# A hybrid decoder step on one core: tile 1's output matmuls spread over the query jobs, and the last tile's sums finished by halves of the columns

## The chip, the cores and the metric

The kernel runs on one core of a Trainium2 chip. The time is that of one execution on the device, in microseconds (us), median of three. A core has TensorE (PE, matmuls; PEld is its weight loads), VectorE (DVE), ScalarE (ACT), GpSimd (POOL), SyncE (SP, which here only issues DMAs), and sixteen DMA engines that all queues share. Engines run their own instruction lists in order and meet at semaphores.

## What is computed

A hybrid decoder layer (attention and a state-space branch) for 512 prompt tokens and 8 sample tokens, followed by a product-key expert layer. Only its second half is touched by the change:

```python
yp = yp + mp                      # mp, ms: output projection m @ w_out of the mixer
ys = ys + ms
yp = yp + _peer(_rmsnorm(yp, norm_ffn[l]), peer_w_q[l], peer_keys1[l], peer_keys2[l], peer_u[l], peer_v[l])
ys = ys + _peer(_rmsnorm(ys, norm_ffn[l]), ...)
y_prompt = _rmsnorm(yp, norm_final)
y_sample = _rmsnorm(ys, norm_final)

# _peer, for a token: 8 heads, 2 x 128 keys
q = (hc @ w_q).reshape(PEER_CHUNK, PEER_HEADS, PEER_QDIM)
s1, s2 = scores of the two halves of q with the two key tables
v1, i1 = lax.top_k(s1, 16);  v2, i2 = lax.top_k(s2, 16)
sc, ci = lax.top_k(all 256 sums v1 + v2, 16)
e = i1[ci // 16] * 128 + i2[ci % 16]          # 128 expert rows a token
g = softmax(sc)
out = sum over e of g * gelu(u_tab[e] . hc) * v_tab[e]
```

## The kernel before

Tokens lie in five tiles of 128: tiles 0 to 3 are the prompt, tile 4 the eight samples. Two stages matter, each a block with its own semaphores and closed by a barrier of all engines (`open_block`, L95). The order inside a block is written out by hand: each engine runs a Python function that emits its instructions, and where a piece goes is set by small constants such as `OUT_AT`.

**stage_route** (L1667) works on tiles 0 and 1. `out(n)` on TensorE is one half of columns of the output projection of one tile: n = 0, 1 are tile 0, n = 2, 3 tile 1, eight matmuls each (two instructions a matmul in the trace, L1788). VectorE's `add(n)` (L1919) puts it onto the residual y1. ScalarE squares a tile (`square`, L1849) and takes the root (`root`), VectorE's `variance` and `scale` (L1929) give the normed h. `turn(t)` transposes it (L1800), ScalarE's `keep_turned` (L1858) copies it to hT. Then come 28 jobs, `JOBS`, each a query matmul group (`queries`, L1812) and scores against the keys (L1831), with copies by ScalarE (L1845). There are 16 half heads (hh). Jobs 0 to 11 are half heads of tile 0 alone, jobs 12 to 15 are of both tiles together (256 wide), jobs 16 to 27 of tile 1 alone. VectorE takes the best 16 of each half head of tile 0 (`best16`, L1587 to L1594) in the loop `for hh in range(HH)`, and after each of the `PORTIONS` the best 16 sums (`choose_best`, L1604). The indices of all but the last portion are worked out on POOL (L1724 to L1737), the last by VectorE (`choose_index`, L1619 to L1629). When all are there, ScalarE takes exponents (job `EXP_AT`), VectorE normalises (L1637 to L1639), TensorE turns indices and gates (`turn_choice`, behind job `CHOICE_AT`), ScalarE stores them in idxT and gateT (L1652, L1653), and POOL issues the first four gathers of expert rows (L1744). ScalarE, POOL and VectorE also split h into three bf16 parts (`split_high`, `split_middle`, L1712, L1714, L1970, L1972), which SP stores to h_split (`store_rows`, L1759) for the next stage. SP loads the weights of the queries (L1501), and at the end two pieces of late weights (L1773) and the gain of the norm (L1775).

**stage_experts** takes 130 batches. A batch is four gathers by POOL (L2097), each of 128 rows of 8 KB (u and v of an expert), the broadcast of h (L2203), four dot products on VectorE (L2462), a gelu on ScalarE, weights (`weights`, L2356), and sixteen matmul instructions that sum the v rows into acc (`combine`, L2309): the first eight fill columns 0 to 511, the others 512 to 1023. The routing of tiles 2 to 4 is done between the batches in the first half of this stage. When a tile is through, `finish` (L2366 add, L2369 variance, L2375 scaling) and ScalarE's `square` and `root` (L2503, L2507) give its output, and SP stores it (L2110; L2114 for the samples, batches 128 and 129).

Of the kernel before, what the change touches and what calls it, by code (L numbers as in the profile page):

```python
# [21 lines left out]
ALU = mybir.AluOpType  # L22
ACT = mybir.ActivationFunctionType
# [7 lines left out]
P = 128  # L31
D = 1024
KT = D // P
# [6 lines left out]
TILES = 5  # L40
# [9 lines left out]
EPS = 1e-6  # L50
# [14 lines left out]
TOPK = 16  # L65
# [1599 lines left out]
def stage_route(nc, io, S):  # L1665
# [3 lines left out]
    PORTIONS = ((0, 2), (2, 2), (4, 2), (6, 1), (7, 1))  # L1669
# [3 lines left out]
    OUT_AT, SQUARE_AT, ROOT_AT = 3, 5, 6  # L1673
    TURN_AT = 7
    EXP_AT, CHOICE_AT = 21, 26
    with ExitStack() as ctx:
# [27 lines left out]
        def _(pool):  # L1704
# [12 lines left out]
            for i, (first, count) in enumerate(PORTIONS[:-1]):  # L1717
                pool.wait_ge(E["halved"], i + 1)
                n = count * TOPK
                f = R.fi[:, 2:2 + 2 * count].rearrange("p (h w) a -> p h w a", w=2)  # L1720
                hit = R.hit[:, 0:count]
                terms = hit.rearrange("p h k a -> p (h k) a")
                hl, hf, pick = (x[:, :, TOPK:TOPK + n] for x in (R.hl, R.hf, R.pick))
                link(pool.tensor_copy(R.fi[:, 2:2 + 2 * count], R.iu[:, 0, 2 * first:2 * (first + count), :]))  # L1724
# [23 lines left out]
        def _(sp):  # L1748
# [13 lines left out]
            for c in range(4, len(JOBS) // 2):  # L1762
                sp.wait_ge(E["q_done"], 2 * (c - 3))
                load_route(sp, io, S, c)
                if c == 6:
                    store_rows(0)
                if c == 8:
                    sp.wait_ge(E["stored"], 16)
                    sp.wait_ge(E["normed"], EARLY)
                    load_rows(sp, S, 0, S.first_rows)  # L1770
            sp.wait_ge(E["done"], 2 * EARLY)
# [4 lines left out]
            store_rows(1)  # L1776
# [3 lines left out]
        def _(pe):  # L1780
# [42 lines left out]
            out(2, 4, KT)  # L1823
            for j, (hh, t0, t1) in enumerate(JOBS):
# [9 lines left out]
                if j == OUT_AT:  # L1834
                    out(3)
# [8 lines left out]
        def _(act):  # L1844
# [37 lines left out]
            for j, (hh, t0, t1) in enumerate(JOBS):  # L1882
# [21 lines left out]
                if j == CHOICE_AT - 1:  # L1904
                    split_middle(1)
# [6 lines left out]
        def _(dve):  # L1912
# [29 lines left out]
            for hh in range(HH):  # L1942
                dve.wait_ge(E["s_kept"], kept_by[hh] + 1)
                best16(dve, link, [(R.v[:, 0, hh, :], R.iu[:, 0, hh, :], s[:, hh, :])])
                for i, (first, count) in enumerate(PORTIONS):
                    if hh == 2 * (first + count) - 1:
# [7 lines left out]
                        hl = R.hl[:, :, TOPK:TOPK + n]  # L1954
# [3 lines left out]
                if hh == 0:  # L1958
                    add(2)
                if hh == OUT_AT:  # L1960
                    add(3)
# [13 lines left out]
def stage_experts(nc, io, S):  # L1975
# [12 lines left out]
    with ExitStack() as ctx:  # L1988
# [13 lines left out]
        ss = sb("ss", [P, TILES + LATE])  # L2002
# [10 lines left out]
        ss2, rstd2 = ss[:, TILES:], rstd[:, TILES:]  # L2013
# [20 lines left out]
                 "h_stored", "room_free", "moved")  # L2034
# [153 lines left out]
        def _(pe):  # L2188
# [108 lines left out]
            def combine(B):  # L2297
# [7 lines left out]
                for h in range(2):  # L2305
                    for c in range(BATCH):
# [5 lines left out]
                                         start=(r == 0), stop=(r == (LANE if n < TILES - 1 else LAST_B) - 1))  # L2312
                last.then_inc(E["v_used"], 1)
# [31 lines left out]
        def _(dve):  # L2345
# [148 lines left out]
            weights(len(batches) - 1)  # L2494
            finish(TILES - 2, 2)
            for part in range(3):
                finish(TILES - 1, part)

        @block.scalar
        def _(act):  # L2500
# [103 lines left out]
            square(TILES - 1)  # L2604
# [202 lines left out]
```

## Time and profile before

| | us |
|---|---|
| median of 3 runs | 2030.96 (2028.79 to 2032.86) |
| the profiled execution's own time | 2034.55 |
| its span, first to last instruction | 2032.8 |
| stage_route, from its first matmul to the experts' first | 505.9 to 618.9 |
| stage_experts | 618.9 to 2032.8 |

Busy shares over the whole span are PE 76%, DVE 64%, POOL 33%, ACT 14%. They mix stages with different limits; the stage in question has to be read from its own stretch. In the rows below, a line of a timeline is: start, duration, engine, line of the kernel, operation, tensors, shapes, count, and in brackets how long the engine had been idle and what ended that. POOL's DMA_INDIRECT rows are the time to issue a gather, not to move it.

### The profile page before, as it was taken

The page shows a single profiled execution, that of the slowest core. Times are in us where ns is not written, and L with a number is a line of the kernel's source. Part 1 is how long each engine was busy: PE and PEld are TensorE (multiplying, and loading weights), DVE is VectorE, ACT ScalarE, POOL GpSimd, SP SyncE. Part 2 cuts the span into 40 slices and gives each one's busy share as a digit, 9 for nine tenths or more (in the row PEclk, how much of TensorE's full clock was granted, in tenths as well). Part 3 has the DMA queues.
Part 4 walks back from the last instruction along what each step waited for, and adds up shares of the span by engine and source line. Part 5 has one row for each costly group of instructions (what it writes and reads, how often), then busy time and mean ns, then how long its engine had stood idle before and what let it go on. Part 6 is the DMA issues. An engine that isn't in the chain of part 4 may idle for free.

```text
span 2032.8 us, 22490 instructions
## 1 busy us (share of the span) xinstructions
PE 1548.4 (76%) x7517; PEld 684.5 (34%) x7517; DVE 1295.6 (64%) x3113; ACT 294.3 (14%) x723; POOL 677.9 (33%) x832
## 2 busy tenths in 40 slices
PE   6999789999986888886787866665666666666665
PEld 5447575637683445441343411110001111111110
DVE  5999627532475787745577896458886445454545
ACT  3001135421222222201111101000000000000000
POOL 4930003400283333233332333333333333333332
PEclk9999787999997888996777866556666555666656
DMA  5322433364669999999999999999999999999997
GB/s 190 104 82 87 135 102 127 111 252 160 216 226 382 421 413 407 412 413 418 413 374 414 393 401 413 422 414 414 406 403 420 413 418 414 415 415 410 418 414 293
DMA packets 141591, 668.59 MB, mean 329 GB/s; under 512 B 17252, under 2 KB 50724, under 8 KB 71524
## 3 DMA queue, kind: packets, MB, share of 16 engines
q0 software_dynamic: 74880, 545.29, 65.5%
q1 hardware_dynamic: 66596, 121.85, 17.5%
q8 instruction: 61, 1.00, 0.2%
q14 instruction: 54, 0.44, 0.1%
HBM read 659.95 MB, written 19.65 MB: 334 GB/s over the span
## 4 chain that ended last, share of the span: by engine, by line
DMA 32%; PE 19%; DVE 8%; issue 7%; POOL 3%; ACT 0%; DVEq 0%; POOLq 0%; ACTq 0%
DMA ex_uv<-in_peer_uv,idxT 20%; DMA w_out<-in_peer_uv,idxT 12%; PE ex_acc L2309 10%; PE ex_hb L2203 4%; DVE ex_uv L2462 2%; POOL ex_uv L2097 2%; PE ex_late L2228 2%; POOL w_out L2097 1%; PE ex_late L2276 1%; DVE w_out L2462 1%; PE ex_pick L2228 1%; PE ex_late L2243 1%; DVE ch_iu L1590 1%; PE ex_late L2256 1%; DVE ch_ci L1590 1%
## 5 line engine op out<-in xcount | busy, mean ns | idle before, releaser
L2203 PE MATMUL ex_hb<-ffn_gain,spread 24*128 24x512 bf16 x1040 | 355.8, 505 | 404.5 <-DVE ex_uv L2462 260.9
L2462 DVE SCALAR_TENSOR_TENSOR ex_uv<-ex_uv,ex_hb 128x1024 f32<-128x1024 f32 x344 | 416.3, 1219 | 312.9 <-DMA ex_uv<-in_peer_uv,idxT 278.8
L2097 POOL DMA_INDIRECT ex_uv<-in_peer_uv,idxT x344 | 325.4, 946 | 612.7 <-PE ex_acc L2309 523.0
L2462 DVE SCALAR_TENSOR_TENSOR w_out<-w_out,ex_hb 128x1024 f32<-128x1024 f32 x176 | 213.1, 1219 | 164.7 <-DMA w_out<-in_peer_uv,idxT 123.6
L2203 PEld LDWEIGHTS ex_hb<-ffn_gain,spread 24*128 24x128 bf16 x1040 | 54.0, 99 | 740.1 <-DVE ex_uv L2462 398.5
L2309 PE MATMUL ex_acc<-ex_uv,wts 128*32 128x512 f32 x1376 | 276.3, 946 | 0.0
L2097 POOL DMA_INDIRECT w_out<-in_peer_uv,idxT x172 | 161.5, 939 | 297.5 <-PE ex_acc L2309 258.2
L2592 ACT ACTIVATE ex_gelu<-ex_dots 128x4 f32<-128x4 f32 x130 | 26.7, 205 | 1087.3 <-DVE ex_uv L2462 725.8
L2309 PE MATMUL ex_acc<-w_out,wts 128*32 128x512 f32 x704 | 139.9, 938 | 0.8 <-DVE wts L2356 0.8
L2309 PEld LDWEIGHTS ex_acc<-ex_uv,wts 128*32 128x32 f32 x1376 | 47.7, 147 | 160.3 <-issue 160.3
L756 POOL TENSOR_TENSOR at_prob<-at_prob,at_coef 128x256 f32<-128x256 f32 (+3 forms) x32 | 40.1, 1253 | 120.6 <-DVE at_coef L866 120.5
L2276 PE MATMUL ex_late<-hx,sgT 128*128 128x264 f32 x256 | 67.9, 423 | 0.0
L1812 PE MATMUL ro_pq<-hT,w_q 128*128 128x128 f32 (+1 forms) x448 | 61.3, 290 | 0.8 <-ACT hT L1858 0.8
L1812 PEld LDWEIGHTS ro_pq<-hT,w_q 128*128 128x128 f32 x448 | 56.8, 192 | 3.4 <-issue 2.0
L2276 PEld LDWEIGHTS ex_late<-hx,sgT 128*128 128x128 f32 x256 | 51.9, 208 | 16.8 <-issue 7.1
L2309 PEld LDWEIGHTS ex_acc<-w_out,wts 128*32 128x32 f32 x704 | 24.4, 147 | 85.2 <-issue 82.7
L2228 PE MATMUL ex_late<-hx,sgT 128*128 128x264 f32 x128 | 39.1, 471 | 9.1 <-DVE ex_small L2394 9.1
L297 DVE TENSOR_TENSOR vc<-pr_x,pr_tab 128x512 f32<-128x512 f32 x64 | 43.0, 731 | 0.6
L624 PE MATMUL pr_yp<-vc,pr_c_pad 128*32 128x256 f32 x256 | 35.4, 425 | 8.8 <-DVE vc L297 8.8
L297 DVE TENSOR_TENSOR pr_x<-pr_bu,pr_tab 128x512 f32<-128x512 f32 x64 | 39.6, 678 | 1.2 <-PE pr_bu L611 1.2
L1705 POOL MEMSET y<- 128x1024 f32 x1 | 1.0, 952 | 110.6 <-POOLq L99 110.6
L572 PE MATMUL pz<-gate_ring,vc 128*128 128x512 f32 (+1 forms) x96 | 36.6, 534 | 0.0
(500 smaller groups left out, 2177.7 us busy)
## 6 DMA issues: line engine op xcount, KB each, us to landing
sgT<-in_late_w SPq DMA_DIRECT2D x24, 1024.0 KB, 9.1
w_q<-in_peer_w_q SPq DMA_DIRECT2D x14, 1024.0 KB, 6.3
gate_ring<-in_w_in SPq DMA_DIRECT2D x6, 2048.0 KB, 9.5
ex_uv<-in_peer_uv,idxT POOLq DMA_INDIRECT x344, 13.6
ks_rows<-in_ks_pages SPq DMA_DIRECT2D x64, 64.0 KB, 2.2
vs_rows<-in_cache_v_sel SPq DMA_DIRECT2D x64, 64.0 KB, 2.1
vc<-in_vc_pages SPq DMA_DIRECT2D x64, 64.0 KB, 2.1
gate_ring<-in_kc_pages SPq DMA_DIRECT2D x64, 64.0 KB, 2.1
```

What stands on the lines that cost most here:

```text
L297: tt = lambda o_, x_, y_, op: dve.tensor_tensor(o_, x_, y_, op)
L572: last = pe.matmul(ps[j % 3][0:m_, 0:n], of, ring[:, c % 2, k, 0:n], start=(k == 0), stop=(k == KT - 1))
L624: last = pe.matmul(yp[strip(n), (p // 2) % 2, 0:SPAN], c_pad[:, part, n, :], zb[:, s % 2, j, e, :], start=(j == 0), stop=(j == 3))
L756: pool.tensor_tensor(prob[:, b, :, 0:n], prob[:, b, :, 0:n], coef[:, b, :].unsqueeze(2).broadcast_to([P, NKV, n]), ALU.mult).then_inc(E["s ...
L1590: ins = dve.max_index(idx[:, part], vals[:, part], x)
L1812: last = pe.matmul(pq[:, j % 2, P * t0:P * t1], w[:, c % 4, k, P * m:P * m + P], S.hT[:, k, P * t0:P * t1], start=(k == 0), stop=(k == KT ...
L2097: pool.indirect_dma_start(slot(s).rearrange("p j n -> p (j n)"), None, table, bass.IndirectOffsetOnAxis(ap=S.idxT[:, t:t + 1], axis=0))\
L2203: last = pe.matmul(hb[s % 2][:, CHUNK * h:CHUNK * h + CHUNK], spread[p, k % LOAD, :], h_rows[p, l % 2, CHUNK * h:CHUNK * h + CHUNK], start ...
L2228: last = pe.matmul(bank[i][:, 0:LATE_TOK], w[:, k, col], S.hx[:, k, :], start=(k == 0), stop=(k == KT - 1))
L2276: last = pe.matmul(late[:, 0:LATE_TOK], w[:, k, P * (j % 2):P * (j % 2) + P], S.hx[:, k, :], start=(k == 0), stop=(k == KT - 1))
L2309: last = pe.matmul(acc[LANE * g:LANE * g + LANE, CHUNK * h:CHUNK * h + CHUNK], wts[:, s % (2 * BATCH), LANE - 1 - r:2 * LANE - 1 - r], slo ...
L2462: dve.scalar_tensor_tensor(out=rows_, in0=rows_, scalar=1.0, in1=hb[s % 2][:], op0=ALU.mult, op1=ALU.mult, accum_out=dots[:, B % 2, c:c + ...
```

## The change

In stage_route:

- The last two portions, of one head each, become one of two heads: POOL works out three portions, VectorE the indices of the last two heads. The scratch buffers that POOL uses start two heads further on, since VectorE's own part needs two.
- out(2)'s second half goes behind job 3, out(3)'s halves behind jobs 5 and 7 (before: out(2)'s second half ahead of the second query, all of out(3) behind job 3). VectorE adds them behind half heads 4 and 7 (before 0 and 3).
- The square of tile 1 moves from job 5 to 9, the root from 6 to 10, the transposes (`TURN_AT`) from behind job 7 to behind job 10, next to the first job that needs them. The variance and scaling on VectorE follow.
- The exponents go from job 21 to 19, the turn of the choice from 26 to 22. The middle part of tile 1's split goes from job 25, one ahead of the choice, to job 23, one behind it.
- SP stores tile 1's split ahead of the two late weight pieces and the gain, not behind them.

In stage_experts, at the very end: the samples' last sum is added in two halves of 512 columns, the first as soon as the first eight matmul instructions are through (new semaphore `half_used`), both ahead of tile 3's scaling. ScalarE squares each half into its own column of ss, and VectorE puts the two sums together in two small steps.

```diff
-    PORTIONS = ((0, 2), (2, 2), (4, 2), (6, 1), (7, 1))
+    PORTIONS = ((0, 2), (2, 2), (4, 2), (6, 2))
...
-    OUT_AT, SQUARE_AT, ROOT_AT = 3, 5, 6
-    TURN_AT = 7
-    EXP_AT, CHOICE_AT = 21, 26
+    OUT_AT = {3: (2, 4, KT), 5: (3, 0, 4), 7: (3, 4, KT)}
+    SQUARE_AT, ROOT_AT, TURN_AT = 9, 10, 10
+    EXP_AT, CHOICE_AT = 19, 22
...
# SyncE, end of stage_route
                     load_rows(sp, S, 0, S.first_rows)
+            store_rows(1)
             sp.wait_ge(E["done"], 2 * EARLY)
             for p in range(2):
                 sp.dma_start(S.late_ring[:, p, :], io["late_w"][p]).then_inc(S.late_w[p], 16)
             gain = S.uT[:, :, 0:EARLY_TOK]
             sp.dma_start(gain, io["norm_ffn"][0, :]...).then_inc(S.ffn_in, 16)
-            store_rows(1)
             sp.wait_ge(E["stored"], 32)
# TensorE
             queries(0)
-            out(2, 4, KT)
             for j, (hh, t0, t1) in enumerate(JOBS):
...
-                if j == OUT_AT:
-                    out(3)
+                if j in OUT_AT:
+                    out(*OUT_AT[j])
                 if j == TURN_AT:
                     turn(1)
# ScalarE
-                if j == CHOICE_AT - 1:
+                if j == CHOICE_AT + 1:
                     split_middle(1)
# VectorE
-                if hh == 0:
+                if hh == 4:
                     add(2)
-                if hh == OUT_AT:
+                if hh == 7:
                     add(3)
                 if hh == SQUARE_AT - 1:
                     variance(1)
...
# stage_experts, TensorE, in combine(B)
+                    if B == len(batches) - 1 and h == 0:
+                        last.then_inc(E["half_used"], 1)
# VectorE, end
             weights(len(batches) - 1)
+            n = TILES - 1
+            r, y = rstd[:, n:n + 1], S.y1[:, home(n), :]
+            dve.wait_ge(E["moved"], 16 * BATCH)
+            dve.wait_ge(E["half_used"], 1)
+            dve.tensor_tensor(y[:, 0:CHUNK], acc[:, 0:CHUNK], y[:, 0:CHUNK], ALU.add).then_inc(E["summed"], 1)
+            dve.wait_ge(E["v_used"], ends[n])
+            dve.tensor_tensor(y[:, CHUNK:], acc[:, CHUNK:], y[:, CHUNK:], ALU.add).then_inc(E["summed"], 1)
             finish(TILES - 2, 2)
-            for part in range(3):
-                finish(TILES - 1, part)
+            dve.wait_ge(E["squared"], TILES)
+            link(dve.tensor_scalar(r, ss[:, n:n + 1], 1.0 / D, EPS, ALU.mult, ALU.add))
+            dve.wait_ge(E["squared"], TILES + 1)
+            dve.scalar_tensor_tensor(out=r, in0=ss[:, TILES + LATE:], scalar=1.0 / D, in1=r,
+                                     op0=ALU.mult, op1=ALU.add).then_inc(E["var"], 1)
+            finish(n, 2)
# ScalarE, end
-            square(TILES - 1)
+            halves = split(S.y1[:, home(TILES - 1), :])
+            for half in range(2):
+                act.wait_ge(E["summed"], TILES + half)
+                at = TILES - 1 if half == 0 else TILES + LATE
+                act.activation(junk[:, 2 * half:2 * half + 2], halves[:, 2 * half:2 * half + 2], ACT.Square,
+                               accum_out=ss[:, at:at + 1]).then_inc(E["squared"], 1)
             root(TILES - 1)
```

TensorE around the transposes of tile 1, before (ro_ps is the output projection, ro_pq a query, ro_pss a score, ro_pt the transposes):

```order
L1831 MATMUL ro_pss<-w_keys,ro_q 128x128
L1800 MATMUL ro_pt<-ident,h 128x128 x8
L1812 MATMUL ro_pq<-hT,w_q 128x128 x8
L1831 MATMUL ro_pss<-w_keys,ro_q 128x128
L1812 MATMUL ro_pq<-hT,w_q 128x128 x8
```

Four narrow queries stood between the transposes and the first wide one (128x256). The same place after the change, from out(3)'s second half on:

```order
L1788 MATMUL ro_ps<-w_out,sgT 128x512 x4
L1812 MATMUL ro_pq<-hT,w_q 128x128 x8
L1830 MATMUL ro_pss<-w_keys,ro_q 128x128
L1812 MATMUL ro_pq<-hT,w_q 128x128 x8
L1830 MATMUL ro_pss<-w_keys,ro_q 128x128
L1812 MATMUL ro_pq<-hT,w_q 128x128 x8
L1830 MATMUL ro_pss<-w_keys,ro_q 128x128
L1800 MATMUL ro_pt<-ident,h 128x128 x8
L1812 MATMUL ro_pq<-hT,w_q 128x256 x8
L1830 MATMUL ro_pss<-w_keys,ro_q 128x128
```

The wide query, which needs the turned tile, now stands right behind the transposes.

SyncE's queue at the end of stage_route (sgT holds the late weights, uT the gain), as the difference:

```order
 L1501 DMA w_q<-in_peer_w_q 128x8x256 [waits pr_z_kept] x5
-L1773 DMA sgT<-in_late_w 128x2048 [waits pr_gain_in]
-L1773 DMA sgT<-in_late_w 128x2048
-L1775 DMA uT<-in_norm_ffn 128x4x256
 L1759 DMA h_split<-ro_part 128x3072 [waits pr_rot_done]
+L1774 DMA sgT<-in_late_w 128x2048 [waits pr_gain_in]
+L1774 DMA sgT<-in_late_w 128x2048
+L1776 DMA uT<-in_norm_ffn 128x4x256
```

The three loads stood ahead of the store and of its wait, and now stand behind both.

VectorE at the end of the program (ex_acc is the sum of a tile), before:

```order
L2369 TENSOR_SCALAR ex_rstd<-ex_ss 128x1
L2356 TENSOR_TENSOR wts<-ex_gelu,gateT 128x4
L2372 RECIPROCAL ex_rstd<-ex_rstd 128x1
L2375 SCALAR_TENSOR_TENSOR y<-y,ex_rstd,uT 128x1024
L2366 TENSOR_TENSOR y<-ex_acc,y 128x1024
```

and after:

```order
L2370 TENSOR_SCALAR ex_rstd<-ex_ss 128x1
L2357 TENSOR_TENSOR wts<-ex_gelu,gateT 128x4
L2500 TENSOR_TENSOR y<-ex_acc,y 128x512
L2502 TENSOR_TENSOR y<-ex_acc,y 128x512
L2373 RECIPROCAL ex_rstd<-ex_rstd 128x1
L2376 SCALAR_TENSOR_TENSOR y<-y,ex_rstd,uT 128x1024
L2505 TENSOR_SCALAR ex_rstd<-ex_ss 128x1
L2507 SCALAR_TENSOR_TENSOR ex_rstd<-ex_ss,ex_rstd 128x1
L2373 RECIPROCAL ex_rstd<-ex_rstd 128x1
L2376 SCALAR_TENSOR_TENSOR y<-y,ex_rstd,uT 128x1024
```

The add, in two halves, moved ahead of tile 3's reciprocal and scaling.

## Rows read from the trace of the kernel before

**Rows 1.** Table of stretches: busy us (count), granted clock, DMA share, GB/s

```profile
core 0: us, PE busy (x) PEld busy (x) DVE busy (x) ACT busy (x) POOL busy (x), PEclk, DMA share, GB/s
619.00:700.00 81.00, 68.30 (x300) 34.73 (x297) 57.73 (x158) 19.62 (x27) 29.18 (x31) 0.81 0.99 408
1180.00:1600.00 420.00, 264.82 (x990) 43.22 (x982) 301.74 (x771) 22.27 (x62) 154.73 (x164) 0.61 1.01 411
```

**Rows 2.** Timeline of POOL, 603 to 620: start, us, instruction, idle before

```profile
604.25 1.16 POOL L1744 DMA_INDIRECT w_out<-in_peer_uv,idxT  x1 [1.33 <-ACT gateT L1653]
...
608.20 0.94 POOL L1744 DMA_INDIRECT w_out<-in_peer_uv,idxT  x1 [0.30 <-issue]
619.49 0.94 POOL L2097 DMA_INDIRECT ex_uv<-in_peer_uv,idxT  x1 [10.35 <-issue]
```

**Rows 3.** DMA view, 604 to 619: queue, packets, MB, share

```profile
q0 software_dynamic: 576, 4.19, 70.7%
```

**Rows 4.** Timeline of TensorE in stage_route

```profile
505.93 19.00 PE L1788 MATMUL ro_ps<-w_out,sgT 128*128 128x512 f32 x40 [2.53 <-PEq L99]
...
529.19 3.60 PE L1788 MATMUL ro_ps<-w_out,sgT 128*128 128x512 f32 x8
...
562.47 3.62 PE L1812 MATMUL ro_pq<-hT,w_q 128*128 128x256 f32 x16
...
582.09 1.95 PE L1812 MATMUL ro_pq<-hT,w_q 128*128 128x128 f32 x16
...
603.07 0.41 PE L1645 MATMUL ro_pt<-ident,ch_eg 128*128 128x128 f32 x2 [0.71 <-POOL ch_eg L1737]
```

**Rows 5.** Timeline of VectorE in stage_route

```profile
535.22 0.29 DVE L1587 MAX8 ch_v<-ro_s 128x8 f32<-128x128 f32 x1 [9.87 <-ACT ro_s L1845]
...
543.18 0.69 DVE L1604 TENSOR_TENSOR ch_work<-ch_v 128x512 f32<-128x512 f32 x1
...
550.05 0.29 DVE L1587 MAX8 ch_v<-ro_s 128x8 f32<-128x128 f32 x1 [0.84 <-ACT ro_s L1845]
...
554.10 1.28 DVE L1929 SCALAR_TENSOR_TENSOR h<-y,ro_rstd,ffn_gain 128x1024 f32<-128x1024 f32 x1
...
591.85 0.17 DVE L1619 CAST ch_fi<-ch_iu 128x32 f32<-128x32 uint32 x1
...
596.84 0.38 DVE L1639 TENSOR_TENSOR ch_eg<-ch_eg,ch_den 128x128 f32<-128x128 f32 x1
```

**Rows 6.** Timeline of SyncE's DMA issues, end of stage_route

```profile
586.49 1.30 SPq L1773 DMA_DIRECT2D sgT<-in_late_w  x2
...
600.98 0.33 SPq L1759 DMA_DIRECT2D h_split<-ro_part  x1
```

**Rows 7.** DMA view, 742 to 746: a late weight load beside gathers

```profile
q1 hardware_dynamic: 110, 0.90, 54.1%
q0 software_dynamic: 112, 0.80, 48.2%
```

**Rows 8.** Table of stretches: start of stage_route, and the barrier

```profile
506.00:507.00 1.00, 1.00 (x2) 0.48 (x3) 0.96 (x2) 1.00 (x1) 1.00 (x4) 0.50 0.21 20
509.00:510.00 1.00, 1.00 (x3) 0.38 (x2) 0.00 (x0) 0.00 (x0) 0.00 (x0) 0.93 1.01 397
617.50:619.00 1.50, 0.12 (x2) 0.16 (x4) 0.00 (x0) 0.16 (x1) 0.00 (x0) 0.50 0.00 0
```

**Rows 9.** Timeline of all engines in the tail

```profile
2022.35 1.92 PE L2309 MATMUL ex_acc<-w_out,wts 128*32 128x512 f32 x16 [0.85 <-DVE wts L2356]
...
2023.84 1.28 DVE L2375 SCALAR_TENSOR_TENSOR y<-y,ex_rstd,uT 128x1024 f32<-128x1024 f32 x1
2025.04 1.22 DVE L2366 TENSOR_TENSOR y<-ex_acc,y 128x1024 f32<-128x1024 f32 x1
...
2026.29 1.06 ACT L2503 ACTIVATE oT<-y 128x1024 f32<-128x1024 f32 x1 [2.68 <-DVE y L2366]
...
2028.09 1.28 DVE L2375 SCALAR_TENSOR_TENSOR y<-y,ex_rstd,uT 128x1024 f32<-128x1024 f32 x1
```

More of the change, by code:

```diff
@@ L1719, in _ @@
                 n = count * TOPK
-                f = R.fi[:, 2:2 + 2 * count].rearrange("p (h w) a -> p h w a", w=2)
+                f = R.fi[:, 4:4 + 2 * count].rearrange("p (h w) a -> p h w a", w=2)
                 hit = R.hit[:, 0:count]
                 terms = hit.rearrange("p h k a -> p (h k) a")
-                hl, hf, pick = (x[:, :, TOPK:TOPK + n] for x in (R.hl, R.hf, R.pick))
-                link(pool.tensor_copy(R.fi[:, 2:2 + 2 * count], R.iu[:, 0, 2 * first:2 * (first + count), :]))
+                hl, hf, pick = (x[:, :, 2 * TOPK:2 * TOPK + n] for x in (R.hl, R.hf, R.pick))
+                link(pool.tensor_copy(R.fi[:, 4:4 + 2 * count], R.iu[:, 0, 2 * first:2 * (first + count), :]))
                 pool.tensor_copy(hf, hl).then_inc(E["places_read"], 1)
@@ L1953, in _ @@
                         n = count * TOPK
-                        hl = R.hl[:, :, TOPK:TOPK + n]
+                        hl = R.hl[:, :, 2 * TOPK:2 * TOPK + n]
                         dve.tensor_scalar(hl[:, 0], R.ci[:, 0:n], 4, None, ALU.logical_shift_right)
@@ L2001, in stage_experts @@
         split = lambda x: x.rearrange("p (k n) -> p k n", k=4)
-        ss = sb("ss", [P, TILES + LATE])
+        ss = sb("ss", [P, TILES + LATE + 1])
         rstd = sb("rstd", [P, TILES + LATE])
@@ L2012, in stage_experts @@
         thirds = small[:].bitcast(BF16).rearrange("p (j n) -> p j n", j=3)
-        ss2, rstd2 = ss[:, TILES:], rstd[:, TILES:]
+        ss2, rstd2 = ss[:, TILES:TILES + LATE], rstd[:, TILES:]
         room = S.R.s1[:].rearrange("p h n -> p (h n)")
@@ L2033, in stage_experts @@
                  "o_done", "o_kept", "sq2", "var2", "root2", "h_ready", "t_done", "t_kept", "hi", "r1", "mid", "lo",
-                 "h_stored", "room_free", "moved")
+                 "h_stored", "room_free", "moved", "half_used")
         E = {n: sem(n) for n in names}
```

## The prediction

> **What bounds the kernel now.** First the table of stretches, for who is busy when. From 619 us to the end the sixteen DMA engines are full: share 0.99 at 619 to 700 and 1.01 at 1180 to 1600, with TensorE's granted clock down at 0.61 and VectorE waiting [rows 1]. The 130 batches of expert rows (4.19 MB each) set the pace there, so whatever delays the first gathers delays all. I take such a shift as one to one.
>
> Then the POOL timeline at the hand-over between the two stages. The four first gathers go out at 604.25 to 608.20 and the next not before 619.49 [rows 2]; they move 4.19 MB [rows 3], the DMA engines are idle at 617.5 to 619 [rows 8], and the experts' block opens at about 618.5. Nothing else is unfinished after 607, so I read that the barrier lets go when the four gathers have landed: 14.2 us from the first issue. Two numbers thus matter in the route stage: when the first gather is issued, and how fast the four move. TensorE's and VectorE's timelines tell what the issue waits for: the transposes of the choice at 603.07, ready last by POOL [rows 4]; VectorE's own part is over at 597.2 (596.84 and 0.38) [rows 5].
>
> **The start of the stage (gain, then given back).** The second half of out(2), 3.60 us of matmuls, stands ahead of the second query job [rows 4]. Moved behind job 3 it lets VectorE begin its first head at 531.8 in place of 535.22 [rows 5]. A head costs 1.8 us (four of them and one add take 535.22 to 543.18), the choice of two heads 5.3 us (543.18 to 550.05, less an add of 0.69 and 0.84 of waiting) [rows 5]. TensorE's narrow job is 2.0 us (1.95 and the rest of a score) [rows 4]. Walking both engines forward in the new order: heads 0 to 3 end at 539.5, head 6 waits 1.6 us for its score (two half outputs of 3.4 us are now between the jobs), the second choice ends at 559.8, and only then, at 560.5, has VectorE added out(3).
>
> **The new wait.** Tile 1's square waits for that add; it is 1.25 us on ScalarE (2026.29 shows one, with 0.19 for reading its sum [rows 9]), and the variance stands behind head 8, the scaling (1.28 us, with its reciprocal 1.4 [rows 5]) behind head 9. So tile 1 is scaled at 565.7. Before, scaling began at 554.10 [rows 5], long before anyone needed it. Now turn(1) comes right behind score 10, at 562.0, and TensorE waits 3.7 us for it; 0.6 us more goes ahead of score 10, since ScalarE stands in the square. Then come 0.9 us of transposes and 0.8 us for the copies, which earlier had a job to hide under. The first wide job starts at 567.6, where it was 562.47 [rows 4]. VectorE's head 11, whose score stands behind this wide job, waits 4.4 us. All of the early gain is spent there.
>
> **The end of the stage.** From the first wide job to the choice's transposes was 40.6 us (562.47 to 603.07), with 0.7 of waiting for POOL [rows 4]. The choice now stands behind job 22, not 26: four narrow jobs less, 8.0 us. TensorE reaches it at 567.6 + 31.9 = 599.5. VectorE is nearly as late: head 15 ends at 587.5, its last choice of two heads takes 5.2, the index of two heads 4.9 (before 4.4 for one, 591.85 to 596.28, but beside POOL's work; POOL is finished now), normalising 0.9: 598.9 [rows 5]. POOL's fourth portion, 11 us, is gone, and its third ends near 593, so POOL is no longer last. By this walk alone the first gather goes at 599.5 + 1.18 (603.07 to 604.25 [rows 2, 4]) = 600.7, which is 3.6 us earlier.
>
> Here the granted clock comes in. TensorE would be idle 4.3 us around 563 with one short score in it. At the stage's beginning, after 2.53 us of idleness [rows 4], the granted clock was 0.50, that is 1.2 GHz, and came back by 509 to 510, some 3 us after work had begun [rows 8]. The same at 565 slows the transposes and the first wide job: 1.2 GHz over 3 us of work costs half of it, 1.5, over both pieces up to 3. I take 2.0 (bounds 0 and 3). TensorE and VectorE are both behind it, as head 11 waits for it. First gather: 602.7, **-1.6 us** (bounds -3.6 and -0.6).
>
> **The moved loads.** SP gives out two late weight pieces (1 MB each) and the ffn gain (0.5 MB) at 586.49, and tile 1's split, 0.79 MB (128 x 3072 bf16), at 600.98 [rows 6]. Now the three stand behind store_rows(1). Its wait for lo queues them until VectorE's last piece of the split, which comes after normalising, the subtraction, ScalarE's middle copy (now behind keep_choice) and the last subtraction: about 605.3. So 2.1 + 0.5 MB that used idle DMA time now meet the gathers, and the store too, which earlier went ahead of them.
>
> What a gather loses beside such a load shows at 742 to 746: 0.90 MB for SP's queue, 0.80 MB for POOL's [rows 7]. With equal shares: data starts at 604.4 (1.7 us behind the first issue), 0.35 MB are gone when SP's store begins at 606 (an estimate, with gathers 1.3 us apart [rows 2]); the store and both pieces, 2.9 MB, then move with 2.9 MB of gathers at 0.42 MB/us, 13.8 us; the last 0.95 MB run beside the gain (at least 2.3 us, at most 3.4; I take 2.6). Last byte at 622.4, 19.7 us after the first issue against 12.9 before (604.25 to about 617.1): +6.8. If the gathers keep 60% it is +5.4; if 65%, +4.5. Nothing of this comes back later, as there the engines are full; only the gain's rest fits in the idle 3 us at the barrier. I take **+5.7 us** (bounds +4.5 and +7.0; a gain is excluded, since the bytes move in any order).
>
> The Trainium skill, "DMA: Bandwidth & Descriptors", section on queues, rings and completion order, says that each DMA engine goes round between the queues that have work, one packet at a time. By that rule 8 KB pieces of both queues share equally, which gives the 6.8; the row at 742 to 746 agrees. It speaks against this change: a load put on another queue does not stand behind the gathers, it goes between them.
>
> **The tail.** Before: weights, 1.92 us of matmuls from 2022.35, tile 3's scaling 2023.84 to 2025.12, then add 1.22, square 1.25, and 0.6 of small steps before the last scaling at 2028.09 [rows 9]. Now the first half is added at about 2023.4 (0.69 us), the second at 2024.4 to 2025.1; ScalarE squares the halves meanwhile (0.8 each, done by 2025.9); tile 3's scaling runs 2025.1 to 2026.5; two small VectorE steps (0.4), the root and reciprocal (0.5), the last scaling starts at 2027.4. That is **-0.7 us** (bounds -1.0 and 0: if the clock is at 1.2 GHz there, the matmuls end as late as 2026 and the adds only change places with the scaling). Tile 3's store goes out 1.4 us later but still 2 us before the last one.
>
> **Sum.** -1.6 + 5.7 - 0.7 = +3.4 us. The profiled execution was 2034.55 us (span 2032.8), 3.6 above the median 2030.96; the difference goes onto the median: 2034.4 us, +0.17%. A measurement of this kernel tells about 0.2% (4.1 us) from no change, so this is "the same", close to "slower".
>
> **Rivals.**
> 1. *The forecast*: the gathers issue a little earlier and share the DMA engines with the moved loads; 2034.4, within 2031 to 2035 as the share and clock vary. Chance 0.45.
> 2. *The clock stays down and the share is equal* (the side of slower). Place: TensorE's idleness ahead of turn(1), then the first wide jobs. Price: 3 us in place of 2, and 6.8 in place of 5.7; -0.6 + 6.8 - 0.7 = +5.5, 2036.5. It decides from 2.7 us of lost clock at an equal share, or 6.4 of sharing at 2. For it: the idleness of 2.5 us that sufficed [rows 4, 8] and the row of 742 to 746. Against it: score 10 breaks the idleness. Chance 0.36.
> 3. *The loads cost nothing*: the barrier does not wait for the gathers' landing but for something on POOL of fixed length, or the experts' first batches have slack. Then -3.6 to -1.6 and -0.7: up to -4.3, 2026.7. Against it: the DMA share of 0.99 right from 619 [rows 1] and the idle engines at 617.5 [rows 8]. Chance 0.12.
> 4. *The change doesn't do what it says*: tile 1's halves and the tail move, but both ends are set elsewhere (the choice stays behind POOL, the tail behind tile 3's scaling): 0 to +6 from the moved loads alone; spread over the cases above, 0.07.
>
> **How the numbers follow.** Likeliest is case 1, 2034.4. The range takes case 2 with the full bounds, -0.6 + 7.0 - 0, up to 2037.3, and reaches down into case 3, to 2027.5. Faster by over 0.2% needs case 3 with the clock unhurt: 0.12. Slower by over 0.2%: case 2 and the upper end of 4, 0.38. The rest, 0.50, within.
>
> **What would show it.** VectorE's first head at about 531.8; an idle TensorE of some 4 us ahead of turn(1) with a granted clock of 0.5 behind it, and head 11 waiting; the choice's transposes at 600 to 603, with POOL no longer last; SP's late pieces near 605, and both queues in the DMA view of 606 to 620; POOL's next gather at about 624 in place of 619.49; in the tail two adds of 512 columns ahead of tile 3's scaling, and the last scaling about 5.0 us behind the start of the last matmuls (before 5.74: 2022.35 to 2028.09). It would be wrong if POOL's next gather stands at or before 619: then the loads did not slow the gathers. It would also be wrong if TensorE never waits before turn(1).

## The result and the profile after

The changed kernel ran at a median of 2040.52 us, the kernel before, run beside it, at 2029.73. The ratio is 1.0042 with a 95% interval of 1.0030 to 1.0054: 8.5 us slower (6.1 to 11.0). It is taken over all executions of both kernels except one of the changed kernel, at 5055.45 us, which fell in the chip's slow state; the two medians happen to lie further apart, 10.8 us. A second set of runs of the same kernel gave 1.0043 (1.0029 to 1.0057). The forecast was +3.4 us and 2034.4, its range ended at 2037.3. Both time and range were missed, on the side of slower.

The profiled execution of the changed kernel took 2037.82 us (span 2035.8), only 3.0 more in span than the one shown of before. Two single executions don't settle a few microseconds, so the stages are read from marks that can be compared.

POOL's timeline of the changed kernel (start, duration, engine, line, operation, idle before and what ended it), beside [rows 2]:

```profile
602.06 1.16 POOL L1744 DMA_INDIRECT w_out<-in_peer_uv,idxT  x1 [7.72 <-ACT gateT L1653]
...
606.67 0.94 POOL L1744 DMA_INDIRECT w_out<-in_peer_uv,idxT  x1 [0.30 <-issue]
625.29 0.94 POOL L2096 DMA_INDIRECT ex_uv<-in_peer_uv,idxT  x1 [17.67 <-issue]
```

The gathers go out earlier (602.06, not 604.25), the experts' next one much later (625.29, not 619.49). SyncE's issues, beside [rows 6]:

```profile
506.71 0.37 SPq L1749 DMA_DIRECT2D y<-in_x_prompt  x1
...
566.67 26.54 SPq L1501 DMA_DIRECT2D w_q<-in_peer_w_q  x5
604.34 0.34 SPq L1759 DMA_DIRECT2D h_split<-ro_part  x1
605.04 1.54 SPq L1774 DMA_DIRECT2D sgT<-in_late_w  x2
606.63 1.97 SPq L1776 DMA_DIRECT2D uT<-in_norm_ffn  x1
```

The store and the three loads are all given out behind the first gather. DMA view of the changed kernel, first 608 to 612 us, then 612 to 620, with packets, MB and share of the sixteen engines for each queue (q0 is POOL's, q1 SyncE's), beside [rows 3, 7]:

```profile
q1 hardware_dynamic: 165, 1.02, 63.0%
q0 software_dynamic: 79, 0.62, 36.8%
```

```profile
q0 software_dynamic: 241, 1.73, 51.2%
q1 hardware_dynamic: 237, 1.69, 50.1%
```

From 612 to 620 the queues share equally, packet for packet. Ahead of that SyncE's queue even had more, and at first that was the store (0.79 MB in rows of 6 KB), not the loads. From 608 to 609.5, while the store moves, POOL's queue all but stands still in the DMA view:

```profile
q1 hardware_dynamic: 85, 0.52, 87.6%
q0 software_dynamic: 9, 0.05, 8.0%
```

TensorE's timeline, beside [rows 4]:

```profile
561.23 0.49 PE L1830 MATMUL ro_pss<-w_keys,ro_q 128*128 128x128 f32 x2 [0.45 <-ACT ro_q L1844]
565.05 1.97 PE L1800 MATMUL ro_pt<-ident,h 128*128 128x128 f32 x8 [3.34 <-DVE h L1928]
567.75 5.09 PE L1812 MATMUL ro_pq<-hT,w_q 128*128 128x256 f32 x16 [0.73 <-issue]
...
600.91 0.38 PE L1645 MATMUL ro_pt<-ident,ch_eg 128*128 128x128 f32 x2
```

Here is the new wait, 3.34 us for tile 1's scaling behind 0.45 ahead of score 10, and behind it a first wide job of 5.09 us that was 3.62. In a second execution of the same kernel this job took longer still:

```profile
567.82 6.66 PE L1812 MATMUL ro_pq<-hT,w_q 128*128 128x256 f32 x16 [0.73 <-issue]
```

VectorE's first head and tile 1's scaling:

```profile
531.02 0.30 DVE L1587 MAX8 ch_v<-ro_s 128x8 f32<-128x128 f32 x1 [6.43 <-ACT ro_s L1844]
...
563.67 1.32 DVE L1928 SCALAR_TENSOR_TENSOR h<-y,ro_rstd,ffn_gain 128x1024 f32<-128x1024 f32 x1
```

The table of stretches for that place (busy us of each engine, then the granted clock, DMA share and GB/s), first for this execution, then for a second one of the same kernel:

```profile
570.00:572.00 2.00, 2.00 (x9) 1.73 (x8) 0.00 (x0) 0.00 (x0) 1.84 (x3) 0.85 0.71 238
572.00:574.00 2.00, 2.00 (x12) 1.77 (x12) 0.43 (x3) 0.55 (x2) 1.27 (x5) 1.00 0.00 0
```

```profile
572.00:574.00 2.00, 2.00 (x6) 1.60 (x6) 0.00 (x0) 0.00 (x0) 1.33 (x5) 0.55 0.00 0
574.00:576.00 2.00, 2.00 (x12) 1.79 (x11) 0.77 (x5) 0.55 (x2) 0.00 (x0) 1.00 0.00 0
```

The clock went to half (0.50, 1.2 GHz) and was back at about 570.6 in one execution and 573.8 in the other. So executions of one kernel differ here. They differ at the stage's start too, where no kernel changes anything: before, the granted clock was 0.50 at 506 to 507 [rows 8]; in the changed kernel it was whole:

```profile
507.00:508.00 1.00, 1.00 (x3) 0.41 (x3) 0.96 (x2) 1.00 (x1) 1.00 (x4) 1.00 0.30 29
```

The tail of the changed kernel, beside [rows 9]; the first answer is TensorE's timeline, the second VectorE's:

```profile
2026.22 1.92 PE L2308 MATMUL ex_acc<-w_out,wts 128*32 128x512 f32 x16 [1.08 <-DVE wts L2357]
```

```profile
2027.42 0.69 DVE L2500 TENSOR_TENSOR y<-ex_acc,y 128x512 f32<-128x512 f32 x1 [1.26 <-PE ex_acc L2308]
...
2029.01 1.28 DVE L2376 SCALAR_TENSOR_TENSOR y<-y,ex_rstd,uT 128x1024 f32<-128x1024 f32 x1
...
2031.02 1.28 DVE L2376 SCALAR_TENSOR_TENSOR y<-y,ex_rstd,uT 128x1024 f32<-128x1024 f32 x1
```

**Marks that can be compared.** The stage starts with SyncE's first issue in it (506.71 above). Over all runs of this study it starts between 501.1 and 506.8, although no kernel changes anything ahead of it. From the experts' first gather to the last matmuls of weighted rows takes 1399.4 to 1402.9 us, with no order by kernel. These two make most of the scatter of the times. What lies between them repeats well and belongs to the kernel. All figures are us, each a difference of starts in the timelines of the kernel's profiled execution; "slow start" means a granted clock of 0.50 in the first microseconds of the stage's matmuls, "low until" the time behind the stage's start at which the clock that fell at TensorE's wait was whole again (worked out from the means in the table of stretches).

| kernel | stage start | start to first gather | first to next gather | start to next gather | granted clock |
|---|---|---|---|---|---|
| before | 505.88 | 98.37 | 15.24 | 113.61 | slow start |
| tail only | 501.52 | 96.79 | 15.19 | 111.98 | whole |
| loads only | 501.10 | 96.79 | 19.38 | 116.17 | whole |
| changed | 506.71 | 95.35 | 23.23 | 118.58 | low until 63.9 |
| changed again | 506.77 | 96.91 | 23.88 | 120.79 | low until 67.0 |
| loads back | 506.31 | 98.29 | 18.26 | 116.55 | slow start, low until 68.2 |
| loads early | 506.29 | 96.92 | 19.14 | 116.06 | low until 67.1 |
| outputs earlier | 503.23 | 97.35 | 24.03 | 121.38 | low until 66.9 |
| both of these | 501.58 | 98.61 | 18.82 | 117.43 | slow start, low until 67.8 |
| gain early | 504.68 | 96.66 | 23.92 | 120.58 | low until 66.5 |
| two more single jobs | 502.07 | 87.58 | 24.13 | 111.71 | whole |
| the same, loads early | 501.89 | 89.03 | 17.91 | 106.94 | slow start |

A slow start costs 98.37 - 96.79 = 1.6 us (the last two lines of the table give 89.03 - 87.58 = 1.5); the fair base is 112.0 without one and 113.6 with one. The changed kernel is then 6.6 to 8.8 us later at the experts' first gather and 0.9 shorter in the tail: +5.7 or +7.9. The second is the usual one: six of the seven profiled executions with TensorE's wait have the longer low clock. +7.9 lies within what the runs say (+6.1 to +11.0, and +5.9 to +11.6 in the second set). The 3.0 us of the two profiled spans hid part of this: before had the slow start (1.6), and the changed kernel's stretch of the experts happened to be 1.9 us shorter.

### The profile page after: what moved, and what is told of

The parts are those of the page before. It is cut to its first block, busy times and chain, and to the rows that moved or that the text cites. A ratio compares the mean times of both kernels' runs of the same rounds, so it can differ in the third digit from the quotient of the medians.

```text
span 2035.8 us, 22474 instructions
## 1 busy us (share of the span) xinstructions
PE 1549.9 (76%) x7517; PEld 687.0 (34%) x7517; DVE 1295.3 (64%) x3111; ACT 294.9 (14%) x725; POOL 670.7 (33%) x814
## 4 chain that ended last, share of the span: by engine, by line
DMA 31%; PE 17%; DVE 9%; issue 8%; POOL 3%; ACT 0%; DVEq 0%; POOLq 0%; ACTq 0%
DMA ex_uv<-in_peer_uv,idxT 19%; DMA w_out<-in_peer_uv,idxT 12%; PE ex_acc L2308 9%; PE ex_hb L2202 3%; DVE ex_uv L2463 2%; POOL ex_uv L2096 2%; PE ex_late L2227 1%; POOL w_out L2096 1%; DVE w_out L2463 1%; DVE ch_iu L1590 1%; PE ex_late L2255 1%; PE ex_late L2275 1%; DVE ch_ci L1590 1%; PE ex_late L2242 1%; DVE ch_sc L1587 1%
## 5 line engine op out<-in xcount | busy, mean ns | idle before, releaser
L2308 PEld LDWEIGHTS ex_acc<-w_out,wts 128*32 128x32 f32 x704 | 24.1, 145 | 83.0 <-issue 80.6
```

The source lines that it names most:

```text
L2308: last = pe.matmul(acc[LANE * g:LANE * g + LANE, CHUNK * h:CHUNK * h + CHUNK], wts[:, s % (2 * BATCH), LANE - 1 - r:2 * LANE - 1 - r], slo ...
```

## The experiments

Ten runs. Time differences are against the kernel before on the same chip, with their 95% intervals.

### The loads put back

```diff
-            store_rows(1)
             sp.wait_ge(E["done"], 2 * EARLY)
 ... (late pieces, gain)
+            store_rows(1)
```

> The changed kernel with one thing undone: the two late pieces and the norm gain are issued again before the second store, on SyncE as in the kernel before. Theory A (the moved loads share the stretch of the four gathers and cost all of the loss and more; the rest of the change gains about 3.0 us at the first gather and 0.9 us at the end): about 4 us faster than the kernel before (2026), gathers issued near 602 and the next gather of the experts' stage 15.2 us behind the first one, as before. Theory B (the changed order of jobs and adds itself costs the 4 us that the profiled execution does not show, somewhere in the experts' stage): within 1.5 us of the kernel before. If neither load nor order costs it but the tail does, this run is as slow as the changed kernel, less 8 us.

Measured: ratio 1.0013 (1.0002 to 1.0025), +2.6 us. The expected gain of 4 us is not there: the first gather comes 98.29 us behind the start, as before (98.37, both with a slow start), and the gather stretch is 18.26, not 15.2. Theory B, which put the cost into the experts' stage, has nothing for it either: the stretch there is 1399.4 us, the shortest of all. SyncE's timeline and then POOL's:

```profile
567.89 27.86 SPq L1501 DMA_DIRECT2D w_q<-in_peer_w_q  x5
595.79 1.30 SPq L1773 DMA_DIRECT2D sgT<-in_late_w  x2
...
606.88 0.33 SPq L1759 DMA_DIRECT2D h_split<-ro_part  x1
```

```profile
604.60 1.16 POOL L1744 DMA_INDIRECT w_out<-in_peer_uv,idxT  x1 [7.72 <-ACT gateT L1653]
...
622.86 0.94 POOL L2096 DMA_INDIRECT ex_uv<-in_peer_uv,idxT  x1 [12.71 <-issue]
```

The order of the two lines is that of before, the time is not. The loads stand behind the last load of w_q, and that one waits for a buffer, so for TensorE's jobs. In the kernel before, SyncE reached them 80.6 us behind the stage's start (586.49 in [rows 6], less 505.88), here 89.5. The DMA view at 598 to 606 us:

```profile
q1 hardware_dynamic: 1382, 3.20, 104.0%
```

SyncE's queue, with w_q and then the loads, holds the engines whole until 606, 1.4 us behind the first gather's issue, and the store follows at 606.88, after the first gather. So theory A is wrong in one half: the loads cost most, but the new order of jobs gains nothing at the first gather, and with it the w_q loads and the store come late, which makes the gather stretch 3.0 us longer. How these 3.0 us split between the loads' end and the store isn't shown.

### The loads moved, in the kernel before

> The kernel before with only the SyncE order changed: second store first, then the two late pieces and the gain. Theory A (moved loads slow the gathers): 8 us slower than before (between 7 and 9), the next gather of the experts' stage 23 us behind the first instead of 15.2. Theory of the prediction (queues share a packet at a time, gathers get 60 per cent): +5.4 us. Rival (the loads cost nothing there; the loss comes from elsewhere): within 1 us of the kernel before.

The edit is the one above in the other direction. Measured: ratio 1.0019 (1.0007 to 1.0031), +3.9 us, and +4.2 from start to next gather (116.17 against 111.98). Theory A's 8 us fails as a price of its own; the prediction's +5.4 is inside the interval. POOL's timeline, SyncE's, and the DMA view at 608 to 610:

```profile
597.89 1.16 POOL L1744 DMA_INDIRECT w_out<-in_peer_uv,idxT  x1 [1.33 <-ACT gateT L1653]
...
617.27 0.94 POOL L2097 DMA_INDIRECT ex_uv<-in_peer_uv,idxT  x1 [14.49 <-issue]
```

```profile
594.62 0.34 SPq L1759 DMA_DIRECT2D h_split<-ro_part  x1
595.32 1.54 SPq L1774 DMA_DIRECT2D sgT<-in_late_w  x2
```

```profile
q0 software_dynamic: 102, 0.70, 84.4%
q1 hardware_dynamic: 106, 0.11, 15.6%
```

In the old order VectorE has the second store ready 3.3 us ahead of the first gather, so the store and part of the loads use engines that would stand idle. In the new order the same store comes 2.3 us behind it. Yet a start ahead of the gathers has a price of its own, and it is not one of sharing: from 599.5 to 602 SyncE's queue moves 136 packets at 100.6% and POOL's none, although its first gather was issued at 597.89. POOL's first packets move 4.1 us or more behind the issue, in the changed kernel under 2 us. Why they wait so long is not shown. The price of the move depends on the rest of the change: 4.2 us in the old order, and in the new 5.0 to 5.6 more in the gather stretch (23.23 and 23.88 against 18.26), and in the times 4.3 us against the kernel with the loads early (below) and 6.1 against the one with them put back (by the ratios, 1.0043 less 1.0022 and 1.0013).

The last view also sizes the packets' part. Once only the gain is left on q1, in packets of 1 KB, q0 has 102 packets to q1's 106, but 0.70 MB to its 0.11. The Trainium skill, "DMA: Bandwidth & Descriptors", section "Queues, rings and completion order", says that an engine takes turns between its queues a packet at a time; this row agrees, by packets as the profile counts them. The stretches above in which one queue moved nearly everything (608 to 609.5 in the changed kernel, 599.5 to 602 here) do not look like turns; whether POOL's queue had packets ready in them, no run shows.

### The tail alone

> The kernel before with only the tail changed: the last tile added, squared and normed by column halves. Theory A (a shorter chain at the very end, 0.9 us): 0.9 us faster than before. Rival B (the changed tail costs some 4 us in the experts' stage by what it moves there): 3 to 4 us slower than before, to be seen in the windows between 700 and 2020 us.

Measured: ratio 0.9991 (0.9979 to 1.0003), -1.8 us with an interval from -4.3 to +0.6. The trace says -0.9: last matmuls to the span's end took 10.47 us before and 9.55 here. Rival B's loss of 3 us or more is excluded.

### The changed kernel again

> The changed kernel once more, unchanged, for its spread and a second profiled execution. Theory A (the profiled execution had a fast experts' stage by chance): again 8 us slower than before in the median, with a profiled execution whose stretch from the experts' first matmul to its last is between 1401 and 1407 us. If there are two ways in which the experts' stage runs, the times fall again in two groups near 2035.5 and 2041.

Measured: 2039.78 us, ratio 1.0043 (1.0029 to 1.0057). The six times are 2036.56, 2037.03 and 2039.73 to 2040.67; ten more in the first set lie at 2035.52 to 2037.82 (four) and 2040.29 to 2043.39 (six). That looks like two groups some 3 us apart, but so few times don't prove it. They are not two ways in which the experts' stage runs: its stretches in the two profiled executions are 1400.9 and 1401.5 us. Whether they are the two lengths of the low clock isn't shown. The profiled execution gives the second line of marks, 2.2 us later than the first: 1.6 at the first gather, for the clock that came back 3.2 us later, and 0.65 in the gather stretch.

### The loads earlier

```diff
+                if c == 11:
+                    sp.wait_ge(E["done"], 2 * EARLY)
+ ... (late pieces, gain)
             store_rows(1)
- ... (late pieces, gain)
```

> The changed kernel with the late pieces and the norm gain issued earlier still: on SyncE ahead of the last two loads of w_q (their buffers are free once the output products of tile 1 are done), so that they neither stand behind the last w_q load nor beside the gathers. Theory C (the stage ends when all bytes queued around the gathers have landed; what the loads cost is the 2.6 MB they put there, at about 0.42 MB a us): the stretch from the first gather to the next gather of the experts' stage falls from 23.2 us to 15.2 plus 1.9 for the store's 0.79 MB, 17.1 us, and the kernel is 6 us faster than the changed one, within 1.5 us of the kernel before. Rival D (the loads slow TensorE's or w_q's work wherever they stand, so that they cost the same earlier): the first gather comes 3 us or more later and the gain is under 3 us.

Measured: ratio 1.0022 (1.0009 to 1.0035), +4.5 us, 4.3 faster than the changed kernel run again by the ratios (4.7 by the marks, 116.06 against 120.79), where 6 was expected; within 1.5 us of the kernel before it is not. SyncE's timeline and POOL's:

```profile
585.91 1.05 SPq L1774 DMA_DIRECT2D sgT<-in_late_w  x2
...
605.49 0.34 SPq L1759 DMA_DIRECT2D h_split<-ro_part  x1
```

```profile
603.21 1.16 POOL L1744 DMA_INDIRECT w_out<-in_peer_uv,idxT  x1 [7.72 <-ACT gateT L1653]
...
622.35 0.94 POOL L2097 DMA_INDIRECT ex_uv<-in_peer_uv,idxT  x1 [13.60 <-issue]
```

The gather stretch is 19.14, from 23.88 in the execution with the same clock; the first gather did not move (96.92 and 96.91). Theory C holds in kind, rival D falls. In size C was 2 us short: 17.1 was expected, with the store's bytes in it. Part of the difference may be a thin trail of last packets (last section); the rest stays open.

### Outputs and adds one job earlier

```diff
-    OUT_AT = {3: (2, 4, KT), 5: (3, 0, 4), 7: (3, 4, KT)}
-    SQUARE_AT, ROOT_AT, TURN_AT = 9, 10, 10
+    OUT_AT = {2: (2, 4, KT), 4: (3, 0, 4), 6: (3, 4, KT)}
+    SQUARE_AT, ROOT_AT, TURN_AT = 8, 9, 10
```

> The changed kernel with tile 1's remaining output products after jobs 2, 4 and 6 (not 3, 5 and 7) and the adds behind heads 3 and 6 (not 4 and 7), square and root one job earlier; the transposes of tile 1 stay behind job 10. Theory E (TensorE's wait of 3.3 us ahead of these transposes takes the clock to 1.2 GHz for 6.8 to 10.2 us, and both together make the last jobs, the last w_q load and the second store late): the wait is under 1 us, the clock stays full between 560 and 590 us, the first gather comes 2 to 4 us earlier behind the stage's start (92 to 94.5 us, not 95.4 to 96.9), the store too, and the kernel is 2 to 5 us faster than the changed one. Rival F (VectorE's 16 heads set the first gather, the adds earlier only move its work): first gather within 0.5 us of 95.4 and the time within 1 us of the changed kernel.

Measured: ratio 1.0039 (1.0026 to 1.0053), +7.9 us, no better than the changed kernel, and the edit did not do what it was to do. TensorE's timeline:

```profile
559.62 0.69 PE L1830 MATMUL ro_pss<-w_keys,ro_q 128*128 128x128 f32 x2 [2.33 <-ACT ro_q L1844]
562.69 0.69 PE L1800 MATMUL ro_pt<-ident,h 128*128 128x128 f32 x2 [2.37 <-DVE h L1928]
```

The wait moved: 2.33 us ahead of score 10, as ScalarE now stood in the root of tile 1 before it copied that job's query, and 2.37 ahead of the transposes. VectorE's pace sets the scaling, so TensorE waits 4.7 us in two pieces in place of 3.8. This run tells nothing on theory E; the ninth does.

### Both edits together

> Both edits together: loads ahead of the last two w_q loads, and no wait ahead of tile 1's transposes. If theories C and E hold and add: 8 to 11 us faster than the changed kernel, 1 to 3 us faster than the kernel before. If they don't add (loads earlier delay w_q at a faster pace of the jobs): no faster than the better of the two alone.

Measured: ratio 1.0016 (1.0003 to 1.0029), +3.2 us: 5.5 faster than the changed kernel by the ratios, not 8 to 11, and not faster than the kernel before. By the marks the gain is that of the early loads (117.43 with a slow start, 116.06 without in the run above); the second edit adds nothing.

### The norm gain alone earlier

> The changed kernel with only the norm gain (0.52 MB in packets of 1 KB) issued early, the two late pieces (2.1 MB in packets of 8 KB) still behind the store. Theory G (queues take turns a packet at a time, so small packets take little from the gathers): the stretch from first gather to next gather shrinks by 0.3 to 0.7 us from 23.2. Rival H (bytes share evenly, whatever the packets): it shrinks by 1.2 us or more.

One execution, 2040.93 us. The gather stretch is 23.92, no shorter than the changed kernel's 23.23 and 23.88. Sharing by bytes (1.2 us or more) has nothing for it; theory G's 0.3 to 0.7 us can't be told from nothing, since two executions of one kernel differ by 0.65.

### Two more jobs on tile 0 first

```diff
-    SPLIT = 12
+    SPLIT = 14
-    SQUARE_AT, ROOT_AT, TURN_AT = 9, 10, 10
-    EXP_AT, CHOICE_AT = 19, 22
+    SQUARE_AT, ROOT_AT, TURN_AT = 9, 10, 12
+    EXP_AT, CHOICE_AT = 20, 23
-                if j == SQUARE_AT:
+                if j == SQUARE_AT + 1:
-                if j == ROOT_AT:
+                if j == ROOT_AT + 1:
```

> The changed kernel with two more jobs on tile 0 alone ahead of tile 1's transposes (heads 12 and 13: 30 jobs, not 28), the transposes behind job 12, square and root in ScalarE's jobs 10 and 11, exponential and choice at jobs 20 and 23. Theory E2 (TensorE's wait for tile 1's scaling and the clock loss behind it are what eats the gain of the new order; VectorE's part alone would allow the first gather 87 to 89 us behind the stage's start): no wait over 1 us ahead of the transposes, full clock between 560 and 600 us, first gather 87 to 90 us behind the start (changed kernel 95.4 and 96.9), the next gather of the experts' stage 23 to 24 us behind it as before, and 6 to 9 us faster than the changed kernel, so within 2 us of the kernel before. Rival F2 (VectorE or the w_q loads set it): first gather not before 94 us, time within 2 us of the changed kernel.

Measured: ratio 0.9989 (0.9977 to 1.0001), -2.2 us. By the ratios that is 11.0 faster than the changed kernel run again, by the marks 6.9 and 9.1 (111.71 against 118.58 and 120.79); 6 to 9 was expected, and the ratios' difference is uncertain by some 4 us. TensorE's timeline, the granted clock, and POOL's timeline:

```profile
560.42 1.09 PE L1800 MATMUL ro_pt<-ident,h 128*128 128x128 f32 x8
562.30 3.69 PE L1812 MATMUL ro_pq<-hT,w_q 128*128 128x256 f32 x16 [0.78 <-issue]
...
588.43 0.44 PE L1645 MATMUL ro_pt<-ident,ch_eg 128*128 128x128 f32 x2
```

```profile
562.00:580.00 18.00, 17.70 (x129) 16.90 (x129) 16.79 (x71) 4.75 (x16) 15.88 (x22) 1.00 0.82 247
```

```profile
589.65 1.16 POOL L1744 DMA_INDIRECT w_out<-in_peer_uv,idxT  x1 [5.88 <-ACT gateT L1653]
...
613.78 0.94 POOL L2096 DMA_INDIRECT ex_uv<-in_peer_uv,idxT  x1 [18.60 <-issue]
```

Theory E2 holds: two narrow jobs, which the stage has to do in some form anyway, fill the time in which VectorE scales tile 1. No wait is left ahead of the transposes, the clock stays at 1.00 and the first wide job takes 3.69 us. The first gather goes 87.58 us behind the start (95.35 and 96.91 in the changed kernel, 96.79 before). That is 7.8 and 9.3 us earlier, and not all of it is the wait and the clock: two wide jobs have become narrow ones, and with one narrow job more ahead of the choice TensorE has some 1.8 us less to do up to there (a wide job follows the next after 3.9 us, a narrow one after 2.0). The wait gone is 3.8, and the clock makes up the rest, 2.2 and 3.7. The gather stretch stays long at 24.13, as it was to be: this kernel still has the loads there.

### The same with the loads early

> The same with the late pieces and the gain issued after w_q load 11 (as in the run with loads early). Theories C and E2 together: first gather 87 to 90 us behind the start, the next one of the experts' stage 17 to 19.2 us behind it, the stage 3 to 6 us shorter than the kernel before's 112.0 and the kernel 4 to 7 us faster than the kernel before with the tail's 0.9 us (2023.5 to 2026.5). If earlier loads get in the way of w_q at this pace: first gather later than in the run without them by 2 us or more.

Measured: 2022.82 us, ratio 0.9971 (0.9960 to 0.9982), 5.9 us faster than the kernel before (3.7 to 8.1), as expected, and some 14.6 faster than the changed one by the ratios. SyncE's timeline and POOL's:

```profile
571.40 1.06 SPq L1774 DMA_DIRECT2D sgT<-in_late_w  x2
...
593.19 0.34 SPq L1759 DMA_DIRECT2D h_split<-ro_part  x1
```

```profile
590.92 1.16 POOL L1744 DMA_INDIRECT w_out<-in_peer_uv,idxT  x1 [5.88 <-ACT gateT L1653]
...
608.83 0.93 POOL L2097 DMA_INDIRECT ex_uv<-in_peer_uv,idxT  x1 [12.37 <-issue]
```

The first gather is at 89.03 with a slow start, the 1.5 us of the slow start behind the run above, so the earlier loads don't hold up w_q. The gather stretch is 17.91, and the experts begin 6.7 us earlier than in the kernel before (106.94 against 113.61, both with a slow start); with the tail that is 7.6, inside the interval. This kernel beats both. The new order of jobs is a good one; what lost time was two places in it.

## Why the prediction was wrong, point by point

**The start of the stage: right.** VectorE's first head was to start 3.4 us earlier (531.8 for 535.22). Behind the stage's start it is 24.31 us in the changed kernel, 29.34 before and 1.6 of that for the slow start: 3.4.

**The new wait: right.** 3.7 us ahead of the transposes and 0.6 ahead of score 10 were forecast, 3.34 and 0.45 measured. Tile 1 was to be scaled 59.8 us behind the start with the slow start, 58.2 without; it was ready at 58.28 (563.67 and 1.32, less 506.71).

**The end of the stage: right in the middle, its upper bound too low.** POOL was no longer last, the choice stood at 600.91. The first gather was forecast 1.6 us earlier, with 2.0 us for the clock, at most 3. Measured against 96.79 it is 1.4 earlier in one execution and 0.1 later in the other, where the low clock lasted 3.2 us longer. The walk without the clock, 3.6 us earlier, came out. The term for the clock did not: beside the run with two more single jobs, whose clock stays whole, the transposes took 1.97 us for 1.09 and the first wide job 5.09 or 6.66 for 3.69, so the clock cost 2.3 us in one execution and 3.9 in the other, for 2.0 and at most 3. The bound of -0.6 fell: the price of the clock is not one value but two, 1.6 us apart, and I had only one such fall in the trace to go by.

**The moved loads: this is the step that failed.** I took +5.7 us, bounds +4.5 and +7.0. The gather stretch went from 15.2 to 23.2 and 23.9, so +8.0 and +8.7, both outside. The term was too small in more than one place. I let the gathers keep nearly 60% against the one row I had ([rows 7]: nearly equal), and this alone is 1.1 us (6.8 at equal shares, as then seen at 612 to 620). The rest, 1.2 to 1.9 us, is what even equal shares leave out. The last packet of the gathers landed 21.1 us behind the first issue (623.12 less 602.06), where the working at equal shares had 19.7. Two things in that stretch are no equal share: at 608 to 609.5 POOL's queue moved 0.05 MB beside the store's 0.52, and its last 26 packets, 0.11 MB, took from 622 to 623.1. How the difference splits between them is not shown. Nor is the whole stretch the price of SyncE's order: with the lines put back it was still 18.26, 3.0 above before, since in the new order the last w_q load itself goes out 7.5 to 9 us later and the store comes behind the first gather. The prediction's sum has no term for that.

**The barrier: right.** In all twelve profiled executions SyncE's first issue of the experts' stage comes 1.3 to 1.5 us behind the last packet of POOL's queue. It is not the loads that are waited for: in the executions where the gain lands last, its packets run to 0.2 to 0.5 us ahead of that issue. Rival 3, with loads that cost nothing, is out.

**The tail: right.** -0.7 forecast, bounds -1.0 and 0; the last scaling stands 4.80 us behind the start of the last matmuls (2026.22 to 2031.02), 5.74 before: -0.9.

**The sum.** -1.4 to +0.1, +8.0 to +8.7, -0.9: +5.7 to +7.9. Rival 2 had the mechanism (clock down for longer, equal share) at +5.5 and 2036.5 with a chance of 0.36. It should have stood first, as the row of 742 to 746 spoke for an equal share and nothing for 60%. The other row named for it was weaker than it looked: the same 2.5 us of idleness ahead of the stage left the clock whole in eight of twelve executions. And the one thing named against it, that score 10 breaks the idleness, did not save the clock. Its own upper end, 7.0 for the loads, was still 1 to 1.7 us short. What is left up to the measured 8.5, 0.6 us with the usual clock, is within the intervals.

## What to carry to other kernels

Price a transfer that moves onto a busy stretch by the bytes that then stand between the start and the end of the transfers waited for, at an equal share, with the worst start in the bounds. A queue's lines keep their order, not their time: find what the line ahead of them waits for. Before giving up a new order of work, fill the one wait in it: two narrow jobs ahead of the transposes were worth 7 to 9 us by the marks (11 by the times) against the same order with the wait.

## What the runs showed of the hardware that was not expected

The cost of one TensorE wait of 3.3 us was set by how long the clock stayed low behind it: in executions of the same kernel the granted clock was back at 570.6 or at 573.8, and the first gather followed 1.6 us apart. That wait took the clock down in all seven executions that have it (3.3 us, or 2.3 and 2.3 to 2.4 with a score between). The 2.5 us of idleness ahead of the stage did so in four of twelve, with nothing changed there.

The sixteen engines were not empty together at the barrier. In the run with loads early, POOL's last gather packets are few for some time before the experts' stage opens at 621.7; the DMA view at 619 to 620 and at 620 to 621:

```profile
q0 software_dynamic: 4, 0.03, 7.8%
```

```profile
q0 software_dynamic: 1, 0.00, 0.1%
```

Four packets and then one: for 2 us the engines are all but idle, and the stage still waits. The last us up to POOL's last packet holds 4 packets here (619.3 to 620.3), in the kernel before 38 (616.4 to 617.4). This barrier opens by the gathers' last packet, not by their bytes.
